# First input block by token halves in three layers of a twelve-layer model block

## What is computed

```python
# conv layers (two of them)
b_gate, c_gate, u = jnp.split(h @ w_in, 3, axis=-1)
y = (b_gate * depthwise_conv3(c_gate * u, conv_w)) @ w_out
# hyena layer
v, x1, x2 = jnp.split(depthwise_conv3(h @ w_in, short_w, short_b), 3, axis=-1)
z = x1 * long_conv(v, 0)
z = x2 * long_conv(z, 1)
y = z @ w_out
# every layer ends in a residual add and a norm; the last three kinds use an rms norm
x = x + y
h = x * rsqrt(mean(x * x) + 1e-6) * g
```

## Time and profile before

| What | Value |
|---|---|
| Median of 3 runs | 2057.42 us (2056.67 to 2057.86) |
| Span of the profiled execution | 2053.3 us |
| Outside the span, median less span | 4.1 us |
| TensorE busy | 1994.9 us, 97% |
| VectorE busy | 1277.7 us, 62% |
| ScalarE busy | 909.9 us, 44% |
| GpSimd busy | 161.9 us, 8% |
| Mean granted TensorE clock | 0.995 |

### The profile page before, as it was taken

One profiled execution on the slowest core, in us unless ns is written; L12 is line 12 of the kernel. 1 busy time (PEld: TensorE's weight loads), 2 busy tenths in 40 slices (PEclk: granted clock), 3 DMA queues, 4 the chain that ended last, 5 costly groups with the idle time before them and its releaser, 6 DMA issues.

```text
span 2053.3 us, 32584 instructions
## 1 busy us (share of the span) xinstructions
PE 1994.9 (97%) x12754; PEld 1615.8 (79%) x12754; DVE 1277.7 (62%) x1623; ACT 909.9 (44%) x1282; POOL 161.9 (8%) x198
## 2 busy tenths in 40 slices
PE   7999999999999999999999999999999999999999
PEld 6689688878678879888878678877767888897887
DVE  7784755477665556655757655576985554575553
ACT  4462344434444434444545454434434444444442
POOL 2152100000010010000002011001100000000000
PEclk9999999999999999999999999999998999999999
DMA  8321365555166655465555257553324555555554
GB/s 302 113 70 38 102 211 184 185 172 179 61 205 204 195 174 172 167 209 188 167 185 192 71 169 224 192 185 133 103 73 132 190 184 187 171 169 185 185 167 150
DMA packets 93040, 335.95 MB, mean 164 GB/s; under 512 B 11230, under 2 KB 11364, under 8 KB 92623
## 3 DMA queue, kind: packets, MB, share of 16 engines
q1 hardware_dynamic: 85824, 311.62, 45.9%
q0 software_dynamic: 7120, 22.95, 4.0%
HBM read 332.43 MB, written 1.05 MB: 162 GB/s over the span
## 4 chain that ended last, share of the span: by engine, by line
PE 87%; DVE 8%; issue 2%; ACT 1%; POOL 1%; DMA 0%; SPq 0%; DVEq 0%; ACTq 0%; POOLq 0%
PE acc L361 42%; PE acc L448 20%; PE acc L419 9%; DVE w_lo L1554 2%; PE acc L920 2%; PE aux L841 1%; PE aux L468 1%; PE aux L625 1%; PE aux L876 1%; POOL rstd L2371 1%; PE aux L908 1%; DVE operand_lo L1575 1%; ACT w_hi L1169 1%; PE acc L612 1%; PE aux L897 1%
## 5 line engine op out<-in xcount | busy, mean ns | idle before, releaser
L1554 DVE TENSOR_TENSOR w_lo<-w_raw,w_hi 128x1024 fp32r<-128x1024 f32 x588 | 717.3, 1225 | 575.1 <-ACT w_hi L1169 570.4
L1169 ACT ACTIVATE w_hi<-w_raw 128x1024 fp32r<-128x1024 f32 x588 | 620.9, 1060 | 792.9 <-PE acc L361 447.9
L361 PE MATMUL acc<-w_hi,operand_hi 128*128 128x512 f32 x1344 | 535.5, 398 | 26.9 <-DVE operand_lo L1720 12.1
L361 PE MATMUL acc<-w_hi,operand_lo 128*128 128x512 f32 x1344 | 526.4, 392 | 0.0
L361 PE MATMUL acc<-w_lo,operand_hi 128*128 128x512 f32 x1344 | 525.9, 391 | 0.0
L361 PEld LDWEIGHTS acc<-w_hi,operand_hi 128*128 128x128 f32 x1344 | 253.7, 189 | 91.3 <-DVE operand_lo L1575 15.3
L361 PEld LDWEIGHTS acc<-w_hi,operand_lo 128*128 128x128 f32 x1344 | 253.2, 188 | 53.5
L361 PEld LDWEIGHTS acc<-w_lo,operand_hi 128*128 128x128 f32 x1344 | 253.9, 189 | 50.3 <-issue 0.5
L448 PE MATMUL acc<-w_hi,hidden_hi 128*128 128x512 f32 x528 | 210.3, 398 | 0.0
L448 PE MATMUL acc<-w_hi,hidden_lo 128*128 128x512 f32 x528 | 208.5, 395 | 0.0
L448 PE MATMUL acc<-w_lo,hidden_hi 128*128 128x512 f32 x528 | 208.4, 395 | 0.0
(11 more groups left out here) (474 smaller groups left out, 2117.2 us busy)
## 6 DMA issues: line engine op xcount, KB each, us to landing
w_raw<-in_weights SPq DMA_DIRECT2D x588, 512.0 KB, 3.4
ln_gain<-in_gains POOLq DMA_DIRECT2D x7, 512.0 KB, 5.0
bias_at<-in_rpb POOLq DMA_DIRECT2D x12, 256.0 KB, 5.5
ln_gain<-in_ln_g POOLq DMA_DIRECT2D x4, 512.0 KB, 4.1
ln_bias<-in_ln_b POOLq DMA_DIRECT2D x4, 512.0 KB, 5.4
vec_rw<-in_vec POOLq DMA_DIRECT2D x3, 512.0 KB, 5.9
l_rw<-in_lora SPq DMA_DIRECT2D x1, 1152.0 KB, 10.4
iclr_rw<-in_xT SPq DMA_DIRECT2D x2, 512.0 KB, 4.5
```

The costliest lines, as they stand in the source:

```text
L361: mm = pe.matmul(acc[:, 2 * pair + t, :], (ah, al)[x][:, kt, t * P:(t + 1) * P], W[w][:, s, kk * 512:(kk + 1) * 512], start=(kt == 0 and ( ...
L1169: act.activation(whi[:, s, :], raw[:, s, :], ACT.Copy).then_inc(w_hi[s], 1)
L1554: dve.tensor_tensor(wlo[:, s, :], raw[:, s, :], whi[:, s, :].bitcast(F32), ALU.subtract).then_inc(w_lo[s], 1)
```

## The change

The block function is split: `channels` issues the matmuls of one quarter for a slice of tokens, and `first_channels` uses it to run the first block of a conv or hyena layer in two passes over its four quarters, tokens 0 to 127 and then 128 to 255, with 128 moving columns in each matmul. The second half of `tok` is turned inside that block, after the third quarter of the first pass. The slots of the four quarters are released in the second pass only, and hyena's inserted filter work (`after`) runs in the second pass too. Ahead of the block two identity matmuls (`keep_busy(2)`) stand where four stood. On ACT and DVE the first tokens' operand is made ahead of the second tokens' norm.

```diff
+        def channels(q, i, pair, tokens):
+            for kk in range(2):
+                kt = 2 * i + kk
+                for c in range(4):
+                    for x, w in PE_PASSES:
+                        mm = pe.matmul(acc[:, 2 * pair + c // 2, (c % 2) * SEQ + tokens.start:(c % 2) * SEQ + tokens.stop],
+                                       W[w][:, (q + i) % SLOTS][:, kk * 512 + c * P:kk * 512 + (c + 1) * P], (ah, al)[x][:, kt, tokens],
...
+        def first_channels(q, backwards=False, after={}):
+            for t in range(TT):
+                for i in range(4):
+                    if i % 2 == 0:
+                        pe.wait_ge(m["operand_ready"], due(m["operand_ready"]))
+                    if t == 0:
+                        pe.wait_ge(w_lo[(q + i) % SLOTS], nth(q + i))
+                    mm = channels(q, i, 0, slice(t * P, (t + 1) * P))
+                    if t == 0:
+                        if i == 2:
+                            turn(tok, 1, halves=True, backwards=backwards)
+                        continue
+                    mm.then_inc(w_used[(q + i) % SLOTS], 1)
+                    if i in after:
+                        after[i]()
...
             turn(tok, 0, halves=True)
-            keep_busy(2 if first else 3)
-            turn(tok, 1, halves=True)
-            keep_busy(2 if first else 1, bank=0)
-            for j in range(6):
+            keep_busy(2)
+            first_channels(q)
+            for j in range(1, 6):
...
             turn(tok, 0, halves=True)
-            keep_busy(3)
-            turn(tok, 1, halves=True, backwards=True)
-            keep_busy(1, bank=0)
             pe.wait_ge(m["ones_set"], due(m["ones_set"]))
             pe.wait_ge(m["dft_built"], due(m["dft_built"]))
+            keep_busy(2)
...
-            if channels and n < LAYER_NORMS:
+            if rms and n < LAYER_NORMS:
                 ahead(q - 4, 1)
+                square(0)
+                ahead(q - 3, 1)
+                square(1)
+                operand(0)
+                ahead(q - 2, 2)
+                operand(1)
+                return
...
                     rms_normed(0)
+                    ahead(q - 3, 1)
+                    operand(0, (0,))
                     rms_normed(1)
-                    both_operands()
-                    ahead(q - 3, 3)
+                    operand(0, (1,))
+                    ahead(q - 2, 2)
+                    operand(1)
...
-            if channels:
-                add(1, 1)
-                rms_normed(1)
-                both_operands()
-                ahead(q - 3, 3)
-            else:
-                operand(0, (0,))
-                add(1, 1)
-                ahead(q - 3, 1)
-                operand(0, (1,))
-                ahead(q - 2, 1)
-                rms_normed(1)
-                ahead(q - 1, 1)
-                operand(1)
+            operand(0, (0,))
+            add(1, 1)
+            ahead(q - 3, 1)
+            operand(0, (1,))
+            ahead(q - 2, 1)
+            rms_normed(1)
+            ahead(q - 1, 1)
+            operand(1)
```

More of the change, by code:

```diff
@@ L404, in first_block @@
                         turn(src, 1, halves=True)
-        def block_channels(q, pair, operand_waits=False, after={}):
-            for i in range(4):
[L410 to L423, removed]
+        def channels(q, i, pair, tokens):
[5 more added lines that the diff above has]
+                                       W[w][:, (q + i) % SLOTS][:, kk * 512 + c * P:kk * 512 + (c + 1) * P], (ah, al)[x][:, kt, tokens],
+                                       start=(kt == 0 and c % 2 == 0 and (x, w) == (0, 0) and tokens.start == 0),
+                                       stop=(kt == KT - 1 and c % 2 == 1 and (x, w) == (1, 0) and tokens.stop == SEQ), skip_group_check=True)
+            return mm
@@ L424, in block_channels @@
+        def block_channels(q, pair, after={}):
+            for i in range(4):
+                pe.wait_ge(w_lo[(q + i) % SLOTS], nth(q + i))
+                channels(q, i, pair, slice(0, SEQ)).then_inc(w_used[(q + i) % SLOTS], 1)
                 if i in after:
                     after[i]()
+        def first_channels(q, backwards=False, after={}):
[4 more added lines that the diff above has]
+                    if t == 0:
+                        pe.wait_ge(w_lo[(q + i) % SLOTS], nth(q + i))
+                    mm = channels(q, i, 0, slice(t * P, (t + 1) * P))
[6 more added lines that the diff above has]
+                        after[i]()
@@ L996, in conv @@
                     pe.wait_ge(freed, due(freed))
-                block_channels(q + 4 * j, j % 2, operand_waits=(j == 0))
+                block_channels(q + 4 * j, j % 2)
             ready = lambda: pe.wait_ge(m["conv_lo_done"], due(m["conv_lo_done"]))
@@ L1136, in hyena @@
             turn(tok, 0, halves=True)
-            keep_busy(3)
-            turn(tok, 1, halves=True, backwards=True)
-            keep_busy(1, bank=0)
             pe.wait_ge(m["ones_set"], due(m["ones_set"]))
             pe.wait_ge(m["dft_built"], due(m["dft_built"]))
+            keep_busy(2)
             for j in range(6):
-                block_channels(q + 4 * j, j % 2, operand_waits=(j == 0), after={i: lambda i=i: inside_block(j, i) for i in range(4)})
+                steps = {i: lambda i=i: inside_block(j, i) for i in range(4)}
+                if j == 0:
+                    first_channels(q, backwards=True, after=steps)
+                else:
+                    block_channels(q + 4 * j, j % 2, after=steps)
             free(m["dft_done"])
@@ L1192, in residual @@
             rms = more and n >= LAYER_NORMS - 1
-            channels = more and layers[n + 1] in ("conv", "hyena")
             def square(t):
@@ L1207, in residual @@
                 return
-            if channels and n < LAYER_NORMS:
+            if rms and n < LAYER_NORMS:
                 ahead(q - 4, 1)
+                square(0)
[5 more added lines that the diff above has]
+                return
             if rms:
                 square(0)
-            if channels:
-                if n >= LAYER_NORMS:
-                    ahead(q - 4, 1)
-                ahead(q - 3, 1)
-                square(1)
-                both_operands()
-                ahead(q - 2, 2)
-                return
             ahead(q - 4, 1)
```

## The result

The changed kernel takes 2075.69 us (median of 4 runs, 2074.21 to 2078.49), the kernel before beside it on the same chip 2057.64 (4 runs, 2056.67 to 2061.96). The ratio is 1.009, with a 95% interval of 1.0077 to 1.0103: 18.05 us slower. I had put 2079.0 with a range of 2071 to 2090.

What follows compares the result with a forecast made beforehand. TensorE was taken as the bound, busy 1994.9 of 2053.3 us. The terms, 29.94 - 9.84 + 2.76 + 0.6 - 1.89 = +21.6 us, added to the median 2057.42 gave 2079.0 us, range 2071 to 2090.

Steps and rivals of the forecast that it cites:

- Term 1: First blocks' matmuls: 192 of 128 columns, 0.112 us apart by their weight loads, replace 96; +9.98 us a block, +29.94 in all.
- Term 4: Hyena's first block: TensorE's wait for `f_w_sb` goes, as DVE has until the second pass; -1.89 us.
- Term 2: Start of the three first blocks: 2.59, 3.71 and 3.54 us earlier, set by two identity calls; -9.84 us together.
- Term 3: Second turn inside each first block: 3 x 0.92, +2.76 us, plus +0.6 for late matmuls after two breaks a layer.
- What costs nothing: Around the first blocks: splits, second operand, slot releases, SP's loads and POOL's work stay in time, adding no wait.
- A: First blocks' matmuls: columns set the pace, 0.066 us apart; 2054.7 us, no change; chance 0.07.
- B: First blocks' matmuls: loads overlap more, 0.08 us apart; +3.2, 2060.6 us; chance 0.06.
- C: First block at the lower clock, +86; chance 0.04.
- D: First blocks: cover fails at pace 0.112, one more stall of up to 2.3 us a layer; +28.5, 2086; chance 0.05.

Runs made afterwards that it cites:

- e2: The kernel before, its orders kept, with only the three first blocks run in two passes of 128 columns; 2085.0 us, ratio 1.012.
- e3: The kernel before, its orders kept, with the first blocks run in four passes of 64 columns; 2263.06 us, ratio 1.0988.
- e8: The kernel before, no halves; later layers' first operand piece made ahead of the second norm, hyena's `f_w_sb` ahead of the last splits; 2052.84 us, ratio 0.999.
- e5: Against the changed kernel, only four of eight K tiles by halves, last three weight splits behind both operands in DVE's list; 2084.52 us, ratio 1.0142.
- second set of runs: The changed kernel run once more, unaltered, for a second profile; 2077.0 us, ratio 1.0085.

## Why the prediction came out right

**Term 1, +29.94.** Right: 0.111 us by the window, 0.1117 by the starts, against 0.112. e2, with this term and next to nothing else, gives +28.1; term 1 less term 4 is +28.05. That it is the load and not a coincidence is shown by 64 columns at the same 0.111 in e3. The Trainium skill, "TensorE: Matmul & The Clock Gate", section "LDWEIGHTS (loading the stationary operand)", has columns/1.2 ns, 107 ns for 128 columns, and the 0.111 agrees with this within 4 ns. The 81 ns of the Trainium skill's section "Back-to-back issue gap" in the same page is not borne out for these 4-byte weights: 0.111 us with 64 and with 128 moving columns.

**Term 2, -9.84.** The block began 3.75 us earlier in hyena (2.78 after the last matmul before it, where it was 6.53) and 3.6 earlier in the second conv layer (2.78, 6.37), against 3.71 and 3.54 predicted. In the first conv layer 2.59 was right in the second profile (2.64) and 1.6 too much in the first, where the identity pair ran at a lower clock.

**Term 3, +3.4.** The turn took its 0.90 inside the block. From the first matmul to the next block it was 22.6 us in the second conv layer, and 28.13 in hyena instead of 19.04. Counted as in term 2, from the second matmul less one spacing, the 22.6 are 22.29 against the 22.62 of 21.50 + 0.92 + 0.2. By their starts, matmuls 74 to 192 of the block are 0.1117 us apart, and 192 of that are 21.44; so the turn and the breaks cost 0.85 instead of 1.12. Across the turn the starts are 0.93 apart, 0.82 more than a spacing; the first matmul behind it is 0.03 late, the first of the second pass not at all. The 0.6 us for late first matmuls, which no row of before gave, wasn't there.

**Term 4, -1.89.** The wait is gone, also in e2 and e8.

**What costs nothing.** Right: no wait for `w_lo`, the operands or the slots in any of the three blocks. The closest was the second tokens' operand: its first low part was ready 1.5 us before the second pass began, in hyena and in the second conv layer. e5 shows that this cover was worth naming: one split in the wrong place, and it failed.

**The rivals.** A (0.066) and B (0.08) are out by the spacing. What C in the chances stands for, a first block at the lower clock (+86), did not happen at 128 columns, with 1.00 granted over all 22.25 us of the block; at 64 columns it did. D did not happen.

**What is left.** The terms are 1.1 us too large: by place, in the profile where no start fell into a slow stretch, +20.5 against +21.6, 0.3 to 0.4 us in each layer, most of it term 3's. The second set of runs has +20.1 by its medians, the first +18.05. The other 2.4 us of the first set lie within the 3 us by which the parts that no edit touches moved in single profiles. What stays open is when a stop in a load-bound stretch costs the clock: the one of e5 was followed by 17 us at half clock twice, and by none in hyena.

Why the change loses, in one comparison: halving the block costs 4 x 2.45 = 9.8 us a layer and starts it 2.6 to 3.75 us earlier.

## What to carry to other kernels

When moving columns are cut while the stationary tiles stay, count the weight loads first: at 256 columns a matmul took 0.120 us here, hardly more than the 0.111 of its load, and every matmul with fewer columns was paid at the load's price. Halve no more of a block than fills the wait, and make sure that the operands' splits stay ahead, since a stop amid such matmuls can cost the clock for much longer than the stop. Before filling a wait with dearer work, look whether the late producer can be moved in its queue; here the two versions that did this are the only ones with a median below the kernel before, by 2.8 and 3.5 us, and only the second is clear of noise.

## What was not expected of the hardware

A run of back-to-back matmuls of 64 columns lost the full clock: 1.00 for the first 3 to 6 us of the block, then 0.50 for 72 to 82 us in each of three layers, though TensorE was busy throughout these stretches. A wait of 1.4 us amid matmuls of 128 columns was followed by about 17 us at half clock in two places out of three. Without any stop, 22.25 us of 128-column matmuls kept the full clock.
